# A ring of four activation pairs and gate blocks on ScalarE's queue in the outputs' loop of a hybrid decoder layer

## The chip, the cores and the metric

The kernel runs on one NeuronCore of one Trainium2 chip. The metric is the device time of one execution in microseconds (us); lower is better. The core has TensorE (PE), VectorE (DVE), ScalarE (ACT), GpSimd (POOL) and SyncE (SP), an on-chip memory with 128 partitions, and 16 DMA engines between that memory and the device's main memory.

## What is computed

One layer on 512 tokens of width 1024: a token mixer (gated spatial mixing beside attention), and then PEER, a retrieval of single-neuron experts. The change lies wholly in PEER:

```python
q = (xt @ w_query).reshape(t, PEER_HEADS, 2, D_HALF)
scores = jnp.einsum('thpd,hpnd->thpn', q, sub_keys)
sv, si = lax.top_k(scores, 16)
...                                   # top 16 of the 256 candidates of each of the 8 heads
gate = jax.nn.softmax(top_s, axis=-1)
# a block of 128 tokens, each with 128 chosen experts of 16384
u = jnp.take(expert_u, ii, axis=0)
a = jnp.einsum('ted,td->te', u, xi)
w = gi * jax.nn.gelu(a, approximate=False)
vv = jnp.take(expert_v, ii, axis=0)
out = jnp.einsum('te,ted->td', w, vv)
```

## The kernel before

The 512 tokens are four tiles of 128. One tile (SPARSE, tile 0) is done as the reference says: GpSimd gathers, for each of the 128 selections, one expert row per token (`gather_rows`, 512 KB a gather) into a ring of eight rows; VectorE multiplies and sums the `expert_u` rows with the tokens (`dot`, 128 of them) and later adds the weighted `expert_v` rows into `y` (`add`, 128 of them). A gather starts when the `dot` or `add` of eight rows before has freed its place.

The other three tiles (384 tokens, DTOK) are done densely over all 16384 experts, in 128 products of 128 experts each (m = 0 to 127), BODY = 8 of them a loop body, so 16 bodies (ITERS).

The gates come first: for each token a 128x128 matrix of gates is built by TensorE from one-hot rows (`hot_rows` on VectorE, `gate_rows` and `copy_built` on ScalarE, `build`), 16 tokens a chunk, eight chunks a tile (d = 0, 1, 2), and stored to `gates_dense` in main memory.

The products' loop: SyncE loads 512 KB of `uT` for each product (`load_u`, four ahead). ScalarE rounds it (`u_hi`), VectorE makes the rest (`u_lo`), TensorE makes 24 matmuls, ScalarE's GELU puts the result in `a_out`, and SyncE stores a pair of two products' activations (384 KB) to `gelu_dense` (`store_a`). The first 64 products lie beside the retrieval and the building of the gates; m = 64 to 127 are bodies 8 to 15 of a loop of their own.

The outputs' loop, 128 steps, again eight a body. For step m: `load_v` brings 512 KB of `expert_v` into one of RAW = 4 places; `load_a` brings a pair of activations back (two steps, A_STEPS = 2) into one of two places of `a_block`; `load_g` brings the gates of a whole body (1536 KB, in runs of 512 bytes) into one of two places of `g_block`. VectorE makes `w_raw` = activations x gates (L1580), ScalarE rounds it to `w_hi` (L873) and the expert rows to `v_hi` (L867), VectorE makes `v_lo` (L1583) and `w_lo` (L1587), and TensorE makes 18 matmuls (L1153, L1154, L1157) into six banks that stay open over all 128 steps. After them come the last residual, a norm and the stores of the output.

All orders are written out by hand; each engine waits on semaphores. All of SyncE's loads and stores are issued in one order on its one queue. In `step` on SyncE a body's first act is `load_g` for the next body; then each step issues `load_v` for four steps on, and each odd step `load_a`, which may only fill the place that the step has just freed:

```python
if r == 0 and not first and not last:
    sp.wait_ge(w_made, m)
    load_g(J + 1, 1 - odd)
...
if r % A_STEPS == 1 and not (last and r >= BODY - 3):
    sp.wait_ge(w_made, m + 1)
    load_a(BODY // A_STEPS * J + (r + 3) // A_STEPS, (r + 3) // A_STEPS % 2)
```

The first loads of the outputs' loop are issued in the middle of body 15 of the products' loop. Of the `dot`s, 32 lie beside the chunks of d = 1 and 2 (two a chunk) and 96 in bodies 8 to 13 (two a product). Of the `add`s, 32 lie in bodies 14 and 15 (two a product) and 96 in bodies 0 to 11 of the outputs' loop (one a step).

Of the kernel before, what the change touches and what calls it, by code (L numbers as in the profile page):

```python
# [25 lines left out]
P = 128  # L26
# [113 lines left out]
def program(nc, x, cT, w_ada, b_ada, norm1_g, w_in, b_f, sg_ln_g, sg_ln_b, sg_wT, sg_bT,  # L140
# [5 lines left out]
    with ExitStack() as ctx:  # L146
# [100 lines left out]
        a_block = shared[:, 4 * D:4 * D + 2 * A_STEPS * DTOK].rearrange("p (b i t) -> p b i t", b=2, i=A_STEPS)  # L247
        w_raw = shared[:, 4 * D + 4 * DTOK:4 * D + 6 * DTOK].rearrange("p (b n) -> p b n", b=2)
        w_hi = shared_f32r("w_hi", 4 * D + 6 * DTOK, [P, 2, DTOK])
        w_lo = shared_f32r("w_lo", 4 * D + 8 * DTOK, [P, 2, DTOK])  # L250
# [59 lines left out]
        a_in = [sem(f"a_in{b}") for b in range(2)]  # L310
# [71 lines left out]
        def _(sp):  # L382
# [91 lines left out]
            with sp.Fori(LOOP_AT, ITERS - 1) as I:  # L474
                for r in range(BODY):
                    loop_product(I, r, True)

# [7 lines left out]
            def load_g(q, b):  # L485
                src = g_dram[:, :, bass.ds(q * (G_STEPS * GROUP), G_STEPS * GROUP)]
                sp.dma_start(g_block[:, b].rearrange("p g i t -> p g (i t)"), src.rearrange("g p n -> p g n")).then_inc(g_in[b], 16)
# [34 lines left out]
            for r in range(BODY):  # L522
                step(0, r, 0, True, False)
            with sp.Fori(0, ITERS // 2 - 1) as K:
                for odd in (1, 0):
                    for r in range(BODY):
                        step(2 * K + 2 - odd, r, odd, False, False)
            for r in range(BODY):
                step(ITERS - 1, r, 1, False, True)
# [97 lines left out]
        def _(act):  # L627
# [225 lines left out]

            with act.Fori(LOOP_AT, ADD_AT) as I:
                for r in range(BODY):
                    loop_product(I, r, True)
            act.wait_ge(dot_done, NSEL)
            nc.scalar.activation(act_w[:, :], act_w[:, :], ACT.Gelu).then_inc(gelu_done, 1)
            for I in range(ADD_AT, ITERS):
                for r in range(BODY):  # L860
                    loop_product(I, r, I < ITERS - 1)
# [13 lines left out]
            def step(J, r, first, last):  # L875
# [6 lines left out]
            act.wait_ge(built, DTOK // BATCH)  # L882
# [775 lines left out]
```

## Time and profile before

| | |
|---|---|
| median of 3 runs | 1815.28 us (1812.93 to 1815.53) |
| the profiled execution | 1814.15 us, its span 1812.4 us |
| TensorE busy | 1620.0 us, 89% of the span |
| VectorE, ScalarE, GpSimd busy | 1259.2, 664.0, 390.6 us |
| mean granted TensorE clock | 0.960 of full speed |
| DMA | 426.15 MB, mean 235 GB/s |

The span is the time from the first to the last instruction of the profiled execution; busy times are sums over it. Times of day in the views are microseconds from the start of the span. In it the last products' loop runs from about 902 to 1164, the outputs' loop from 1185.6 to 1794.6.

### The profile page before, as it was taken

What the parts mean: (1) busy time and instruction counts of PE and PEld (TensorE: products, weight loads), DVE (VectorE), ACT (ScalarE), POOL (GpSimd) and SP (SyncE); (2) the same over time, 40 slices, a digit from 0 to 9 for tenths busy, and PEclk for the clock granted to TensorE, in tenths of its full rate; (3) what the DMA queues carried; (4) which work ended last, traced back from release to release, by engine and by line L of the source; (5) the groups of instructions that cost most, each with busy time, mean ns of one, the idle gap of its engine ahead of it and who ended that gap; (6) DMA issues with size and microseconds to landing.
All of it is one profiled execution on the core that took longest, in us unless ns stands there. A gap on an engine that the chain in (4) does not pass through costs nothing.

```text
span 1812.4 us, 23042 instructions
## 1 busy us (share of the span) xinstructions
PE 1620.0 (89%) x7605; PEld 1306.1 (72%) x7605; DVE 1259.2 (69%) x2268; ACT 664.0 (37%) x1227; POOL 390.6 (22%) x326
## 2 busy tenths in 40 slices
PE   1999988999889999999999999688888888989996
PEld 0454565545489889989999999666666676768784
DVE  6457255339977889988888888666666666766556
ACT  2111133212378269438633333132323222323333
POOL 1103200000010003002366666422222222220000
PEclk9889999999989999999999999889999899999998
DMA  9853500000266459647999999988889787887663
GB/s 357 291 187 141 209 1 1 0 0 20 74 204 227 146 178 324 242 150 264 326 412 413 413 413 412 396 281 275 282 294 327 260 268 276 305 281 237 196 213 111
DMA packets 172763, 426.15 MB, mean 235 GB/s; under 512 B 13068, under 2 KB 62220, under 8 KB 169496
## 3 DMA queue, kind: packets, MB, share of 16 engines
q1 hardware_dynamic: 135808, 291.06, 45.3%
q0 software_dynamic: 36864, 134.23, 20.5%
q8 instruction: 35, 0.57, 0.1%
q14 instruction: 32, 0.26, 0.0%
q10 hardware_dynamic: 24, 0.02, 0.0%
HBM read 372.84 MB, written 52.43 MB: 235 GB/s over the span
## 4 chain that ended last, share of the span: by engine, by line
PE 55%; DVE 18%; DMA 13%; SPq 5%; issue 4%; ACT 4%; POOL 1%; DVEq 0%; ACTq 0%; POOLq 0%
PE bank L1153 7%; DMA shared<-gelu_dense 7%; PE bank L1154 7%; PE bank L1157 7%; PE bank L1097 5%; SPq L479 5%; PE bank L1099 5%; PE bank L1098 5%; PE bank L951 5%; PE bank L1026 3%; PE bank L961 3%; PE bank L1112 3%; DMA hT<-in_expert_u,idx_slot 2%; ACT weights L794 2%; DVE u_lo L1486 2%
## 5 line engine op out<-in xcount | busy, mean ns | idle before, releaser
L1153 PE MATMUL bank<-v_hi,w_hi 128*128 128x512 f32 x768 | 310.2, 404 | 81.9 <-DVE w_lo L1587 81.7
L1097 PE MATMUL bank<-h_hi,u_hi 128*128 128x384 f32 x1024 | 348.9, 341 | 23.0 <-DVE u_lo L1486 23.0
L1098 PE MATMUL bank<-h_lo,u_hi 128*128 128x384 f32 x1024 | 345.0, 337 | 0.0
L1099 PE MATMUL bank<-h_hi,u_lo 128*128 128x384 f32 x1024 | 345.0, 337 | 0.0
L1154 PE MATMUL bank<-v_lo,w_hi 128*128 128x512 f32 x768 | 306.6, 399 | 0.0
L867 ACT ACTIVATE v_hi<-weights 128x1024 fp32r<-128x1024 f32 x128 | 135.5, 1059 | 302.7 <-PE bank L1157 249.0
L1157 PE MATMUL bank<-v_hi,w_lo 128*128 128x512 f32 x768 | 242.0, 397 | 0.0
L1153 PEld LDWEIGHTS bank<-v_hi,w_hi 128*128 128x128 f32 x768 | 149.3, 194 | 123.3 <-DVE v_lo L1583 70.0
L1097 PEld LDWEIGHTS bank<-h_hi,u_hi 128*128 128x128 f32 x1024 | 194.4, 190 | 27.3 <-DVE u_lo L1486 16.6
L1583 DVE TENSOR_TENSOR v_lo<-weights,v_hi 128x1024 fp32r<-128x1024 f32 x128 | 156.5, 1222 | 77.3 <-ACT v_hi L867 75.0
L1486 DVE TENSOR_TENSOR u_lo<-weights,u_hi 128x1024 fp32r<-128x1024 f32 x128 | 156.0, 1223 | 66.8 <-PE bank L1099 65.7
L1098 PEld LDWEIGHTS bank<-h_lo,u_hi 128*128 128x128 f32 x1024 | 194.2, 190 | 0.0
L1099 PEld LDWEIGHTS bank<-h_hi,u_lo 128*128 128x128 f32 x1024 | 194.2, 190 | 0.0
L1580 DVE TENSOR_TENSOR shared<-shared,weights 128x384 f32<-128x384 f32 x128 | 71.0, 555 | 156.6 <-DMA shared<-gelu_dense 144.8
L1154 PEld LDWEIGHTS bank<-v_lo,w_hi 128*128 128x128 f32 x768 | 149.4, 195 | 30.8
L1157 PEld LDWEIGHTS bank<-v_hi,w_lo 128*128 128x128 f32 x768 | 148.0, 193 | 31.9
L611 POOL DMA_INDIRECT shared<-in_expert_u,idx_slot x64 | 87.2, 1362 | 314.0 <-DVE shared L1493 290.5
L774 ACT ACTIVATE u_hi<-weights 128x1024 fp32r<-128x1024 f32 x128 | 134.9, 1054 | 0.0
L611 POOL DMA_INDIRECT hT<-in_expert_v,idx_slot x64 | 78.7, 1229 | 207.2 <-DVE y L1499 198.1
L1473 DVE TENSOR_TENSOR weights<-ada 128x1024 f32<-128x1024 f32 x96 | 111.4, 1221 | 16.3 <-ACT ada L824 12.8
L611 POOL DMA_INDIRECT hT<-in_expert_u,idx_slot x64 | 91.4, 1429 | 135.0 <-DVE hT L1493 65.8
L794 ACT ACTIVATE weights<-weights,ada 128x128 f32<-128x128 f32 x384 | 115.2, 389 | 14.2 <-DVE weights L1473 14.2
(233 smaller groups left out, 2195.9 us busy)
## 6 DMA issues: line engine op xcount, KB each, us to landing
weights<-in_uT SPq DMA_DIRECT2D x128, 512.0 KB
weights<-in_expert_v SPq DMA_DIRECT2D x128, 512.0 KB, 4.8
weights<-in_w_ada SPq DMA_DIRECT2D x12, 2048.0 KB, 9.6
gates_dense<-weights SPq DMA_DIRECT2D x24, 1024.0 KB, 6.4
shared<-gelu_dense SPq DMA_DIRECT2D x64, 384.0 KB
weights<-gates_dense SPq DMA_DIRECT2D x16, 1536.0 KB, 13.4
gelu_dense<-weights SPq DMA_DIRECT2D x32, 384.0 KB
gelu_dense<-final_row SPq DMA_DIRECT2D x32, 384.0 KB
```

The costliest lines, as they stand in the source:

```text
L611: nc.gpsimd.indirect_dma_start(ring(r % ROWS), None, table, bass.IndirectOffsetOnAxis(idx_slot[:, half, r:r + 1], 0))\
L774: nc.scalar.activation(u_hi[:, r % RAW, :], u_raw[:, r % RAW, :], ACT.Copy).then_inc(u_hi_made, 1)
L794: ins = nc.scalar.activation(rows, rows, ACT.Copy, scale=turned[:, half * HTOK // P % 2, 2, token:token + 1])
L867: nc.scalar.activation(v_hi[:, r % 2, :], v_raw[:, r % RAW, :], ACT.Copy).then_inc(v_hi_made, 1)
L1097: nc.tensor.matmul(a, uh[:, k, :], h2_hi[:, :, k, :], start=(k == 0), stop=False)
L1098: nc.tensor.matmul(a, uh[:, k, :], h2_lo[:, :, k, :], start=False, stop=False)
L1099: ins = nc.tensor.matmul(a, ul[:, k, :], h2_hi[:, :, k, :], start=False, stop=(k == KC - 1))
L1153: nc.tensor.matmul(acc, wh, v_hi[:, r % 2, cols], start=begin, stop=False)
L1154: nc.tensor.matmul(acc, wh, v_lo[:, r % RAW, cols], start=False, stop=False)
L1157: ins = nc.tensor.matmul(acc, wl, v_hi[:, r % 2, cols], start=False, stop=end)
L1486: tt(u_lo[:, r % LOW, :], u_raw[:, r % RAW, :], u_hi[:, r % RAW, :].bitcast(F32), ALU.subtract).then_inc(u_lo_made, 1)
L1583: tt(v_lo[:, r % RAW, :], v_raw[:, r % RAW, :], v_hi[:, r % 2, :].bitcast(F32), ALU.subtract).then_inc(v_lo_made, 1)
```

## The change

It has four parts. (1) `a_block` becomes a ring of four pairs (A_RING = 4), so a pair is loaded four pairs (a whole body) ahead of its use; `w_raw`, `w_hi` and `w_lo` move to other addresses to make room. (2) `load_g` moves from SyncE's queue to ScalarE's: in the outputs' loop ScalarE issues it at the start of a body, ahead of its rounding of `w`. (3) The first loads (four of `expert_v`, four pairs, two gate blocks) are issued in body 14, two bodies ahead of the outputs' loop. (4) The work for the sparse tile is spread anew: 48 `dot`s beside all three tiles' chunks, 64 in bodies 8 to 11 (two a product), 16 in bodies 12 and 13 (one a product), none in body 14; eight `add`s in body 15 (one a product) and 120 in bodies 0 to 14 of the outputs' loop (one a step), where `add` now stands between `w_raw` and `v_lo`.

```diff
-DOTS_AT = {1: 0, 2: 2 * CHUNKS}
-DOTS_IN_CHUNKS = 4 * CHUNKS
-ADD_AT = 14
-ADDS_IN_LOOP = 2 * BODY * (ITERS - ADD_AT)
+DOTS_IN_CHUNKS = 6 * CHUNKS
+FEW_DOTS_AT, DOTS_END, ADD_AT = 12, 14, 15
+ADDS_IN_LOOP = BODY * (ITERS - ADD_AT)
+A_RING = 4
...
-        a_block = shared[:, 4 * D:4 * D + 2 * A_STEPS * DTOK].rearrange("p (b i t) -> p b i t", b=2, i=A_STEPS)
-        w_raw = shared[:, 4 * D + 4 * DTOK:4 * D + 6 * DTOK].rearrange("p (b n) -> p b n", b=2)
+        a_block = shared[:, 4 * D:4 * D + A_RING * A_STEPS * DTOK].rearrange("p (b i t) -> p b i t", b=A_RING, i=A_STEPS)
+        w_raw = ada[:, 2 * D:2 * D + 2 * DTOK].rearrange("p (b n) -> p b n", b=2)
...
 SyncE
-            for r in range(RAW):
-                loop_product(ITERS - 1, r, True)
+            with sp.Fori(LOOP_AT, DOTS_END) as I:
+                for r in range(BODY):
+                    loop_product(I, r, True)
             wait_full(sp, "turn", DENSE - 1)
             for b in range(2):
-                sp.wait_ge(g_stored[b], 16 * GROUPS // 2)
-                sp.wait_ge(a_stored[b], 16)
-            load_v(0, 0)
-            load_a(0, 0)
-            load_g(0, 0)
-            for n in range(1, RAW):
-                load_v(n, n)
-            load_a(1, 1)
-            for r in range(RAW, BODY):
-                loop_product(ITERS - 1, r, False)
-            load_g(1, 1)
+                sp.wait_ge(a_stored[b], 16 * A_RING // 2)
+            for r in range(BODY):
+                loop_product(DOTS_END, r, True)
+                if r < RAW:
+                    load_v(r, r)
+                else:
+                    load_a(r - RAW, r - RAW)
+            for r in range(BODY):
+                loop_product(ITERS - 1, r, r < RAW)
...
-            def step(J, r, odd, first, last):
+            def step(J, r, last):
                 m = BODY * J + r
-                if r == 0 and not first and not last:
-                    sp.wait_ge(w_made, m)
-                    load_g(J + 1, 1 - odd)
+                if r % A_STEPS == 1 and not last:
+                    sp.wait_ge(w_made, m + 1)
+                    load_a(BODY // A_STEPS * (J + 1) + r // A_STEPS, r // A_STEPS)
                 if not (last and r >= RAW):
                     sp.wait_ge(v_used, m + 1)
                     load_v(m + RAW, r)
-                if r % A_STEPS == 1 and not (last and r >= BODY - 3):
-                    sp.wait_ge(w_made, m + 1)
-                    load_a(BODY // A_STEPS * J + (r + 3) // A_STEPS, (r + 3) // A_STEPS % 2)
...
 ScalarE
+            for b in range(2):
+                act.wait_ge(g_stored[b], 16 * GROUPS // 2)
+            act.wait_ge(built, DTOK // BATCH)
+            for r in range(BODY):
+                if r % RAW == 0:
+                    load_g(r // RAW, r // RAW)
+                loop_product(DOTS_END, r, True)
+                if r == 0:
+                    act.wait_ge(dot_done, NSEL)
+                    nc.scalar.activation(act_w[:, :], act_w[:, :], ACT.Gelu).then_inc(gelu_done, 1)
+            for r in range(BODY):
+                loop_product(ITERS - 1, r, False)
...
-            def step(J, r, first, last):
+            def step(J, r, odd, first, last):
+                if r == 0 and not first and not last:
+                    load_g(J + 1, 1 - odd)
                 round_w(J, r, first and r < 2)
...
 VectorE, beside the chunks
-                    if d in DOTS_AT:
-                        for q in range(2):
-                            at = DOTS_AT[d] + 2 * c + q
-                            dve.wait_ge(gathered[at % ROWS], 16 * (at // ROWS + 1))
-                            dot(at, at)
+                    for q in range(2):
+                        at = 2 * (d * CHUNKS + c) + q
+                        dve.wait_ge(gathered[at % ROWS], 16 * (at // ROWS + 1))
+                        dot(at, at)
...
 VectorE, step of the outputs' loop
                 if r % A_STEPS == 0:
-                    dve.wait_ge(a_in[r // A_STEPS % 2], 16 * (BODY // A_STEPS // 2 * J + r // A_STEPS // 2 + 1))
+                    dve.wait_ge(a_in[r // A_STEPS], 16 * (J + 1))
...
                    g_block[:, odd, :, r, :], ALU.mult).then_inc(w_made, 1)
+                if adding:
+                    loop_add(J, r)
...
-                if adding:
-                    n = BODY * J + ADDS_IN_LOOP + r
-                    dve.wait_ge(gathered[r % ROWS], 16 * ((NSEL + ADDS_IN_LOOP) // ROWS + 1 + BODY // ROWS * J))
-                    add(n, r)
```

## Rows read from the trace of the kernel before

**Rows 1.** Busy time of each engine in stretches, with clock and DMA

```profile
core 0: us, PE busy (x) PEld busy (x) DVE busy (x) ACT busy (x) POOL busy (x), PEclk, DMA share, GB/s
1185.60:1794.60 609.00, 548.34 (x2304) 444.19 (x2304) 390.63 (x479) 195.25 (x256) 115.08 (x98) 0.95 0.77 261
902.00:1164.40 262.40, 259.91 (x1493) 258.30 (x1492) 221.00 (x281) 87.10 (x122) 172.84 (x139) 1.00 1.03 409
1164.40:1185.60 21.20, 0.00 (x0) 0.00 (x0) 2.76 (x5) 3.17 (x5) 2.23 (x3) 0.58 1.07 367
1143.00:1173.00 30.00, 20.74 (x117) 19.71 (x115) 18.52 (x15) 4.16 (x6) 14.04 (x14) 0.91 1.04 393
1226.40:1589.42 363.02, 313.27 (x1298) 252.69 (x1297) 240.56 (x288) 109.97 (x145) 94.70 (x81) 0.93 0.84 286
1349.50:1386.97 37.47, 34.98 (x146) 27.91 (x145) 26.70 (x32) 12.36 (x17) 10.70 (x9) 0.95 0.92 310
1670.24:1704.17 33.93, 32.55 (x144) 26.67 (x143) 17.39 (x24) 11.78 (x17) 0.00 (x0) 1.00 0.66 214
1704.17:1737.23 33.06, 32.91 (x145) 26.95 (x144) 17.46 (x24) 12.13 (x17) 0.00 (x0) 1.00 0.68 222
```

**Rows 2.** Chain of waits, the last 12 steps of the outputs' loop

```profile
1745.39 0.47 PE bank L1153
...
1794.15 0.47 PE bank L1157 x2
```

**Rows 3.** Waits from 1185.6 to 1794.6: total us, times, longest

```profile
DVE shared L1580 <- DMA shared<-gelu_dense: 144.8, 52, 8.6
...
PE bank L1153 <- DVE w_lo L1587: 81.7, 24, 21.3
...
ACT v_hi L867 <- DMA weights<-in_expert_v: 53.5, 11, 6.6
```

**Rows 4.** Timeline of SyncE's queue, 1223 to 1236: start, us, what

```profile
1223.39 0.40 SPq L487 DMA_DIRECT2D weights<-gates_dense  x1
...
1232.87 0.38 SPq L482 DMA_DIRECT2D shared<-gelu_dense  x1
```

**Rows 5.** The first load issued behind a gate block (L479), at two places

```profile
L479 SPq DMA_DIRECT2D weights<-in_expert_v x1: 5662/5662/5662, 1226.4 to 1226.4; - x1
...
L479 SPq DMA_DIRECT2D weights<-in_expert_v x1: 27654/27654/27654, 1143.6 to 1143.6; - x1
```

**Rows 6.** ScalarE's timeline between the loops

```profile
1182.34 0.49 ACT L782 ACTIVATE final_row<-bank 128x384 f32<-128x384 f32 x1 [26.44 <-DMA gelu_dense<-final_row]
```

**Rows 7.** Issue to landing: gate blocks 1220 to 1640, then v loads 1300 to 1640

```profile
DMA to landing us min/median/max: 10.5/13.5/14.1
...
DMA to landing us min/median/max: 3.4/5.4/9.6
```

**Rows 8.** DMA queues, 1143 to 1173: packets, MB, share of the engines' time

```profile
q0 software_dynamic: 2396, 8.69, 73.9%
q1 hardware_dynamic: 3055, 3.11, 30.0%
```

**Rows 9.** Groups of instructions in the outputs' loop

```profile
L1583 DVE TENSOR_TENSOR v_lo<-weights,v_hi 128x1024 fp32r<-128x1024 f32 x127 | 155.2, 1222 | 70.6 <-ACT v_hi L867 68.3 <-issue 2.2
...
L867 ACT ACTIVATE v_hi<-weights 128x1024 fp32r<-128x1024 f32 x126 | 133.4, 1059 | 302.7 <-PE bank L1157 249.0 <-DMA weights<-in_expert_v 53.5
...
L1587 DVE TENSOR_TENSOR w_lo<-shared,w_hi 128x384 fp32r<-128x384 f32 x127 | 70.0, 551 | 0.0
```

**Rows 10.** VectorE's timeline, the first and last product beside chunks, d = 0 and 1

```profile
519.65 1.23 DVE L1486 TENSOR_TENSOR u_lo<-weights,u_hi 128x1024 fp32r<-128x1024 f32 x1 [1.21 <-PE bank L1099]
...
575.30 1.23 DVE L1486 TENSOR_TENSOR u_lo<-weights,u_hi 128x1024 fp32r<-128x1024 f32 x1 [1.61 <-PE bank L1099]
...
667.92 1.23 DVE L1486 TENSOR_TENSOR u_lo<-weights,u_hi 128x1024 fp32r<-128x1024 f32 x1 [1.21 <-PE bank L1099]
...
728.58 1.23 DVE L1486 TENSOR_TENSOR u_lo<-weights,u_hi 128x1024 fp32r<-128x1024 f32 x1
```

More of the change, by code:

```diff
@@ L309, in program @@
         a_stored = [sem(f"a_stored{b}") for b in range(2)]
[L310 removed]
+        a_in = [sem(f"a_in{b}") for b in range(A_RING)]
         x_in, c_in, small_in, norm1_in = sem("x_in"), sem("c_in"), sem("small_in"), sem("norm1_in")
@@ L517, in step @@
                     load_v(m + RAW, r)
-                if r % A_STEPS == 1 and not (last and r >= BODY - 3):
-                    sp.wait_ge(w_made, m + 1)
-                    load_a(BODY // A_STEPS * J + (r + 3) // A_STEPS, (r + 3) // A_STEPS % 2)
+            with sp.Fori(0, ITERS - 1) as J:
+                for r in range(BODY):
+                    step(J, r, False)
             for r in range(BODY):
[L523 to L529, printed above, removed]
+                step(ITERS - 1, r, True)
             for t in range(NT):
@@ L1542, in _, with loop_product @@
                             hot_rows(HALVES * (d * CHUNKS + c + 1) + h)
-            def loop_product(I, r, more, adding):
+            def loop_product(I, r):
                 if r + 1 < BODY:
                     rest_of_u(I, r + 1)
-                elif more:
+                elif not (isinstance(I, int) and I == ITERS - 1):
                     rest_of_u(I + 1, 0)
-                for q in range(2):
-                    at = 2 * r + q
-                    if adding:
-                        n = 2 * BODY * (I - ADD_AT) + at
-                        dve.wait_ge(gathered[at % ROWS], 16 * (NSEL // ROWS + 2 * BODY // ROWS * (I - ADD_AT) + at // ROWS + 1))
-                        add(n, at)
-                    else:
-                        n = 2 * BODY * (I - LOOP_AT) + DOTS_IN_CHUNKS + at
-                        dve.wait_ge(gathered[at % ROWS], 16 * (2 * BODY // ROWS * (I - LOOP_AT) + DOTS_IN_CHUNKS // ROWS + at // ROWS + 1))
-                        dot(n, at)
@@ L1560, in _, with loop_dot @@
[L1560 to L1570 removed]
+            def loop_dot(before, I, at):
+                dve.wait_ge(gathered[at % ROWS], 16 * (before // ROWS + I + at // ROWS + 1))
+                dot(BODY * I + before + at, at)
@@ new lines, in loop_add @@
+            def loop_add(J, r):
+                dve.wait_ge(gathered[r % ROWS], 16 * ((NSEL + ADDS_IN_LOOP) // ROWS + 1 + J))
+                add(BODY * J + ADDS_IN_LOOP + r, r)
+            with dve.Fori(LOOP_AT, FEW_DOTS_AT) as I:
+                for r in range(BODY):
+                    loop_product(I, r)
+                    for q in range(2):
+                        loop_dot(DOTS_IN_CHUNKS - 2 * BODY * LOOP_AT, 2 * I, 2 * r + q)
+            before = DOTS_IN_CHUNKS + 2 * BODY * (FEW_DOTS_AT - LOOP_AT)
@@ new lines, in _ @@
+            for I in range(FEW_DOTS_AT, DOTS_END):
+                for r in range(BODY):
+                    loop_product(I, r)
+                    loop_dot(before, I - FEW_DOTS_AT, r)
+            for r in range(BODY):
+                loop_product(DOTS_END, r)
+                if r == 2:
+                    dve.wait_ge(gelu_done, 1)
+                    tt(act_w[:, :], act_w[:, :], gate_sparse[:, :], ALU.mult).then_inc(w_ready, 1)
+                    dve.wait_ge(dot_done, NSEL)
+                    dve.wait_ge(w_ready, 1)
+                    nc.vector.memset(y[:, SPARSE, :], 0.0).then_inc(v_added, 1)
@@ L1572, in step @@
+            for r in range(BODY):
+                loop_product(ITERS - 1, r)
+                loop_add(-1, r)
             def step(K, odd, r, first, adding):
@@ L1600, in _ @@
                         step(K, odd, r, False, True)
-            with dve.Fori(adding_bodies // 2, ITERS // 2) as K:
-                for odd in range(2):
-                    for r in range(BODY):
-                        step(K, odd, r, False, False)
+            for odd in range(2):
+                for r in range(BODY):
+                    step(ITERS // 2 - 1, odd, r, False, odd == 0)
             def finish(t):
```

47 lines of the change are left out of this document (15 added, 32 removed).

## Prediction

> **What bounds the kernel now.** I read the busy times by stretch first, because the share of TensorE over the whole span (89%) hides where it idles. In the outputs' loop TensorE is busy 548.3 of 609.0 us, at a mean granted clock of 0.95; in bodies 8 to 15 of the products' loop 259.9 of 262.4; between the two loops it does nothing for 21.2 us [rows 1]. So there are three places, and the outputs' loop is the large one.
>
> What would the loop take with nothing in the way? Its last 12 steps follow on one another: 1745.39 to 1794.15 + 0.47 is 49.2 us, or 4.10 us a step [rows 2]. 128 steps are 525 us, a body of eight 32.8. The loop takes 84 us more: 61 of idle TensorE, and 23 because matmuls behind a stall run at the lower clock. Nine bodies in a row, all with additions and a gate block each, take 363.0 us, 40.3 each; two late bodies without additions take 33.9 and 33.1 [rows 1].
>
> The waits tell what comes last. VectorE waits 144.8 us for `shared<-gelu_dense`, a pair of activations; behind that TensorE waits for `w_lo` (81.7 us, of which 21.3 are the gap between the loops). A second wait runs beside it: ScalarE waits 53.5 us for rows of `expert_v`, 11 times, up to 6.6 us [rows 3].
>
> Why is the pair late? SyncE's queue shows it. The gate block is issued at 1223.39 in 0.40 us. The next load, of `expert_v`, comes 3.0 us later at 1226.40 and its issue takes 5.66 us; only at 1232.87, behind one more, goes the pair out [rows 4, 5]. The block takes 13.5 us to land [rows 7], and the pair is behind it. With two places, no pair can be issued earlier. At the turn of the loops the same thing is larger: with gathers two a product the load behind the first block stands for 27.65 us [rows 5], all of SyncE's stores stand behind it, and ScalarE waits 26.4 us until `gelu_dense<-final_row` has landed and `final_row` may be written again [rows 6].
>
> **The change, part by part.**
>
> *Ring of four pairs.* A pair is issued as soon as its place is free, eight steps (32.8 us) ahead. Even the late pairs of before would have landed 20 us early. That takes away the wait for `gelu_dense`. What is late next is the load of `expert_v`, issued only when its place is free: the place of step m is freed at the end of m, and ScalarE wants the new rows at the end of step m + 2, two steps or 8.2 us later. They land in 5.4 us at the median, 9.6 at most [rows 7].
>
> *Gate block on ScalarE's queue.* On ScalarE the issue costs some 0.40 us, once a body, ahead of `w_hi`. `v_lo` (1.22 us) is being made meanwhile, longer than the 0.40 us, so I cost it at nothing; without that cover it is 14 x 0.4 = 6 us. Behind it on ScalarE stand `w_hi` and the next `v_hi`, and TensorE waits for both. What the block does to SyncE's loads is the open price. If the load behind it was held by its own queue alone, that cost goes to zero. If what holds it is shared by both queues, the load of `expert_v` is still held. No row of before shows a block on another queue. Bounds: a body of 32.8 us from below; from above one with a late load, worked out under the rivals. I take 33.9 us, the slower of the two late bodies [rows 1]. Independently, the engines' DMA share gives the same: 0.84 x 363.0 / 9 = 33.9 us of DMA time a body with additions [rows 1]. The bytes alone would allow less: eight rows' loads and eight gathers of 0.524 MB, four pairs of 0.393 and a block of 1.57 are 11.5 MB, at the 393 GB/s of the stretch 1143 to 1173 29.3 us [rows 1].
>
> The loop then: blocks are fetched in bodies 1 to 14, 14 x 33.9 + 2 x 32.8 = 540.2 us, against 609.0: **-68.8**. The additions are still one a step and VectorE has room for them: 26.8 us of 32.8 at the rate of the nine bodies (240.6 / 9 [rows 1]). That 24 more of them lie here costs only through the DMA time, which the 33.9 holds for all bodies. In the new place `add` comes before `v_lo`: it fills the time in which ScalarE makes `v_hi`, and costs something only where its gather is late.
>
> *First loads two bodies ahead.* Loads for steps 0 to 3 and both blocks have 33 us and more. The last product takes 4.1 us; meanwhile ScalarE's last but one GELU (0.49), `v_hi` (1.06), `v_lo` (1.22) and `w_lo` (0.55) [rows 6, 9] come to 3.3 us, so TensorE goes on nearly without a gap. I leave 1 us of 21.2: **-20.2**. The price is body 14. It moves eight `uT` rows, four of `expert_v`, four pairs out and four in, and two blocks: 12 x 0.524 + 8 x 0.393 + 2 x 1.57 = 12.6 MB in 33 us, 381 GB/s, when 409 is what the loop moved [rows 1]. ScalarE issues the second block 16 us behind the first; if the first is not far enough, ScalarE stands, and with it GELU and `u_hi`, of which some 6 us are hidden by products made ahead. SyncE's `uT` loads are four products ahead. **+2**, bounds 0 and 12.
>
> *Fewer gathers late in the products' loop.* Eight fewer `dot`s or `add`s a body from body 12 on. The loop idles 2.5 us now [rows 1], part of it at the turn from `dot` to `add`, which stays. **-1.2**, bounds 0 and -2.5.
>
> *Sixteen `dot`s beside the chunks of d = 0.* This part costs. A chunk without `dot`s takes (575.30 - 519.65) / 7 = 7.95 us, with two (728.58 - 667.92) / 7 = 8.67 [rows 10]. Eight chunks: 8 x 0.72 = **+5.8**. Bounds 0 (if the one-hot building on ScalarE is the pace) and 16 x 1.22 = 19.5.
>
> Sum: -68.8 - 20.2 + 2 - 1.2 + 5.8 = -82.4, so a span of 1812.4 - 82.4 = 1730.0. This execution took 1.75 us outside its span, 1731.8; the median of the runs is 1.1 above it: **1733 us**, 4.5% less.
>
> **A rule weighed against the rows.** Where two queues have work, the rows 1143 to 1173 show how they share: gathers in 2396 packets and the rest, mostly pieces of the block, in 3055, while the megabytes are 8.69 to 3.11 [rows 8]; so it is by packet, not by byte. The Trainium skill (DMA: Bandwidth & Descriptors, Queues, rings and completion order) says that a DMA engine takes turns between queues a packet at a time; by this rule, the trace agrees, the block on a third queue gets small turns and lands later than 13.5 us, but it delays each packet of the others only by one short one. With 33 us to land, the sum stays.
>
> **Rivals.**
>
> *A. Both queues share what makes the issues wait.* The block is issued on ScalarE about 1.2 us into a step (behind `v_hi`), the path stays taken until 8.7 us after the issue (0.40, 3.0 and 5.66 us make 1223.39 to 1232.06 [rows 4, 5]), that is 9.9 us into it. The load of `expert_v` due at 4.2 goes out then, lands 5.4 later at 15.3, and `v_hi`, `v_lo`, `w_lo` end at 18.2 with the hand-overs, when TensorE wants it at 16.4: 1.9 us late. With a landing of 9.6 it is 6.1. For: the second wait [rows 3] shows such loads late even now. Against: in those cases they also stood behind the block's bytes in one queue. With 1.9 to 6.1 and the low clock behind it, say 3.6 a body, the loop is 525 + 50 = 575, and body 14 some 6 instead of 2: 1812.4 - 34 - 20.2 - 1.2 + 5.8 + 6 + 2.9 = **1772 us**. 
>
> *B. The DMA engines are the bound.* The highest share that a body with additions reached is 0.92 (1349.5 to 1387.0 [rows 1]), so 33.9 / 0.92 = 36.8 us: 15 x 36.8 + 32.8 = 585, hence -24: 1812.4 - 24 - 20.2 - 1.2 + 5.8 + 2 + 2.9 = **1778 us**. For: 0.84 busy at a 40.3 us body. Against: 409 GB/s at a share of 1.03 in the products' loop.
>
> *C. Nothing left in the way.* Bodies of 33.0: 528, body 14 free: **1718 us**.
>
> *D. Slower than before.* ScalarE itself stands at each block until the first two thirds are out, as SyncE's next issue does (8.7 us). `w_hi` then comes at 9.9 us, `w_lo` at 11.2, and TensorE stands 7 us a body and loses 2 more at the low clock: 525 + 14 x 9.4 = 657, and body 14 with two such waits +20: 1812.4 + 48 - 20.2 - 1.2 + 5.8 + 20 + 2.9 = **1868 us**. It decides from about 7 us lost a body. Against: issuing the block took 0.40 us, it was the next one that stood.
>
> **How the numbers follow.** Chances: the forecast (bodies about 33.9, 1724 to 1748) 0.42, A 0.24, B 0.08, C (below 1724) 0.18, D 0.04; 0.04 for something not seen. The forecast's own range is 1724 to 1748. The range over the cases is 1708 to 1772: the low end is C with no cost of body 14 and chunks that hide half of the `dot`s, the high end is the middle of A. A measurement here can tell 0.2% (3.6 us) from no change. All but D and a little of the rest are faster: faster 0.94, same 0.02, slower 0.04.
>
> **What the profile after would show.** Waits for `shared<-gelu_dense` on VectorE gone; between the loops no gap above 2 us; bodies of the outputs' loop 33 to 35 us at a DMA share near 1; nothing on SyncE held 5 us. If A is right, each body has one issue of `expert_v` of 5 us or more just behind ScalarE's block, and ScalarE waits for `weights<-in_expert_v`. If B is right, the block's landing nears 33 us and VectorE waits for `weights<-gates_dense`. If D is right, the issue on ScalarE's queue is long. Chunks of d = 0 should stand 8.7 us apart. The prediction is wrong if the loop's body stays above 37 us or ScalarE loses its lead in body 14.

## The result, and the profile after

The changed kernel takes **1709.07 us** (median of 4, 1705.92 to 1710.63) against 1815.4 before in the same comparison: ratio 0.941, 95% interval 0.9385 to 0.9433, 5.9% faster. The prediction was 1733 with a range of 1708 to 1772. The direction and the mechanism held; the gain is 24 us larger than forecast, and the time lies only 1 us above the low end of the range.

The spans are 1812.4 and 1705.9 us, 106.5 apart. The windows of the changed kernel show where they went (columns as in [rows 1]):

```profile
core 0: us, PE busy (x) PEld busy (x) DVE busy (x) ACT busy (x) POOL busy (x), PEclk, DMA share, GB/s
1163.80:1688.00 524.20, 522.92 (x2306) 432.26 (x2304) 418.87 (x501) 189.63 (x257) 188.40 (x125) 1.00 0.92 326
902.00:1163.80 261.80, 261.80 (x1512) 261.80 (x1511) 180.48 (x234) 91.47 (x128) 113.42 (x100) 1.00 0.97 366
1200.00:1600.00 400.00, 398.91 (x1761) 330.13 (x1760) 327.52 (x390) 144.37 (x195) 165.27 (x110) 1.00 0.99 353
```

The outputs' loop takes 524.2 us where it took 609.0 [rows 1], with TensorE busy in 522.9 of them and the clock at full speed. That is 32.8 us a body, the floor that the prediction read from [rows 2]. It begins at 1163.8, in the same microsecond in which the products' loop ends; the 21.2 us between the loops are gone. The products' loop itself has no idle microsecond left.

The waits from 1170 to 1680 hold no line for `gelu_dense` any more. The wait for rows of `expert_v` is left, smaller than the 53.5 us of [rows 3] and spread over more times. The two lines beneath it are what TensorE waited for in the whole loop, the first before a load of weights, the second before a matmul:

```profile
ACT v_hi L866 <- DMA weights<-in_expert_v: 44.7, 15, 4.7
```

```profile
  DVE v_lo L1595: 2.1, 2
  DVE w_lo L1599: 1.3, 2
```

Of ScalarE's 44.7 us almost nothing reaches TensorE, which is idle for 1.3 of the loop's 524.2 us: rows that come while ScalarE and VectorE still have time in a step cost nothing.

The loads in the loop, landing in us, answer to [rows 7]: first the gate blocks on ScalarE's queue with their issues, then the rows of `expert_v` with theirs from 1200 to 1680.

```profile
L843 ACTq DMA_DIRECT2D weights<-gates_dense x16: 379/401/441, 1093.6 to 1618.9; - x16
...
DMA to landing us min/median/max: 15.6/27.0/28.8
...
L475 SPq DMA_DIRECT2D weights<-in_expert_v x116: 327/333/339, 1200.9 to 1671.8; - x116
...
DMA to landing us min/median/max: 3.1/6.2/10.2
```

A block now lands in 27.0 us instead of 13.5 and has 33. No issue of `expert_v` takes over 0.339 us, where the one behind a block took 5.7 [rows 5]. The queues from 1200 to 1600 (packets, MB, share):

```profile
q1 hardware_dynamic: 21101, 70.50, 47.0%
q0 software_dynamic: 14098, 51.33, 34.6%
q10 hardware_dynamic: 37774, 19.24, 16.9%
```

q10 is ScalarE's queue. It has half of the packets and a seventh of the bytes.

The remaining part of the difference lies before the loop. TensorE's turns of the gates (the last of three transposes, one a tile d) are good marks. Before, then after:

```profile
510.70 0.27 PE L921 MATMUL bank<-ident,gate 128*128 128x128 f32 x1
658.97 0.27 PE L921 MATMUL bank<-ident,gate 128*128 128x128 f32 x1
815.47 0.27 PE L921 MATMUL bank<-ident,gate 128*128 128x128 f32 x1
```

```profile
507.51 0.27 PE L922 MATMUL bank<-ident,gate 128*128 128x128 f32 x1
662.15 0.27 PE L922 MATMUL bank<-ident,gate 128*128 128x128 f32 x1
818.69 0.27 PE L922 MATMUL bank<-ident,gate 128*128 128x128 f32 x1
```

The first mark is 3.2 us earlier though nothing ahead of it changed; over all runs of this study it lies between 506.5 (e2) and 511.8 (e1), so this is scatter. From the first to the second, where the 16 `dot`s were added, it takes 154.6 instead of 148.3 us: +6.4. From the second to the third 156.5 both times. From there to the end of the products' loop (1164.4, then 1163.8) 345.1 instead of 348.9: -3.8. In sum -3.2 + 6.4 - 3.8 - 21.2 - 84.8 = -106.6, which is the 106.5 of the spans within rounding.

### The profile page after: what moved, and what is told of

It reads as the page before. It is cut to its first block, busy times and chain, and to the rows that moved or that the text cites. A ratio compares the mean times of both kernels' runs of the same rounds, so it can differ in the third digit from the quotient of the medians.

```text
span 1705.9 us, 22939 instructions
## 1 busy us (share of the span) xinstructions
PE 1591.9 (93%) x7605; PEld 1291.6 (76%) x7605; DVE 1258.1 (74%) x2268; ACT 658.8 (39%) x1227; POOL 424.5 (25%) x326
## 4 chain that ended last, share of the span: by engine, by line
PE 72%; DVE 18%; ACT 5%; DMA 3%; issue 2%; ACTq 0%; DVEq 0%; SPq 0%
PE bank L1154 10%; PE bank L1158 10%; PE bank L1155 10%; PE bank L1098 8%; PE bank L1100 8%; PE bank L1099 8%; PE bank L952 5%; PE bank L1027 3%; PE bank L962 3%; ACT weights L781 3%; DVE u_lo L1487 2%; PE bank L1044 2%; DVE weights L1474 2%; DVE ada L1403 1%; PE bank L1113 1%
## 5 line engine op out<-in xcount | busy, mean ns | idle before, releaser
L1154 PE MATMUL bank<-v_hi,w_hi 128*128 128x512 f32 x768 | 298.9, 389 | 1.3 <-DVE w_lo L1599 1.3
L1155 PE MATMUL bank<-v_lo,w_hi 128*128 128x512 f32 x768 | 298.8, 389 | 0.0
L1158 PE MATMUL bank<-v_hi,w_lo 128*128 128x512 f32 x768 | 236.6, 389 | 0.0
L1154 PEld LDWEIGHTS bank<-v_hi,w_hi 128*128 128x128 f32 x768 | 144.2, 188 | 31.7 <-DVE v_lo L1595 2.1
L1155 PEld LDWEIGHTS bank<-v_lo,w_hi 128*128 128x128 f32 x768 | 144.2, 188 | 29.9
L1158 PEld LDWEIGHTS bank<-v_hi,w_lo 128*128 128x128 f32 x768 | 144.2, 188 | 29.9
L598 POOL DMA_INDIRECT hT<-in_expert_v,idx_slot x64 | 107.3, 1677 | 159.1 <-DVE y L1500 143.2
L598 POOL DMA_INDIRECT shared<-in_expert_v,idx_slot x64 | 94.9, 1483 | 188.7 <-DVE y L1500 170.2
```

Of the source, the lines that this page charges most:

```text
L598: nc.gpsimd.indirect_dma_start(ring(r % ROWS), None, table, bass.IndirectOffsetOnAxis(idx_slot[:, half, r:r + 1], 0))\
L1154: nc.tensor.matmul(acc, wh, v_hi[:, r % 2, cols], start=begin, stop=False)
L1155: nc.tensor.matmul(acc, wh, v_lo[:, r % RAW, cols], start=False, stop=False)
L1158: ins = nc.tensor.matmul(acc, wl, v_hi[:, r % 2, cols], start=False, stop=end)
```

## The experiments

Ratios are to the kernel before, run on the same chip in the same job. The loop is the outputs' loop, from the start of its first to the end of its last matmul; the gap is TensorE's idle time ahead of it. Both come from one profiled execution of each run, while the median is over four to six.

| run | median us (range) | ratio, 95% | loop us | gap us |
|---|---|---|---|---|
| before | 1815.4 | | 609.0 | 21.3 |
| after | 1709.07 (1705.92 to 1710.63) | 0.941 (0.9385 to 0.9433) | 524.2 | 0 |
| e1, blocks on SyncE | 1744.37 (1740.51 to 1752.68) | 0.959 (0.9564 to 0.9624) | 564.8 | 0 |
| e2, blocks on ScalarE alone | 1785.33 (1782.65 to 1794.69) | 0.984 (0.9799 to 0.9874) | 586.4 | 21.3 |
| e3, no first dots | 1711.01 (1709.27 to 1712.83) | 0.942 (0.9398 to 0.9442) | 523.9 | 0 |
| e4, first loads later | 1710.44 (1708.29 to 1712.77) | 0.942 (0.9393 to 0.9438) | 524.8 | 0 |
| e5, two blocks at once | 1708.49 (1707.88 to 1709.92) | 0.943 (0.9397 to 0.946) | 523.8 | 0 |
| e6, no first dots, late GELU | 1711.37 (1708.96 to 1712.49) | 0.944 (0.9416 to 0.9465) | 523.0 | 0 |
| e7, old spread | 1727.10 (1724.98 to 1730.08) | 0.953 (0.9505 to 0.9556) | 525.8 | 3.8 |
| e8, two more loads | 1743.75 (1739.50 to 1746.21) | 0.961 (0.958 to 0.9648) | 558.5 | 0 |
| e9, second block later | 1704.36 (1700.36 to 1705.92) | 0.940 (0.9384 to 0.9424) | 523.7 | 0 |
| e10, one dot a chunk | 1700.43 (1699.74 to 1704.22) | 0.938 (0.936 to 0.9402) | 524.7 | 0 |
| e11, add behind w_lo | 1707.82 (1706.21 to 1711.79) | 0.943 (0.9404 to 0.9449) | 524.6 | 0 |
| e12, first loads as before | 1723.13 (1722.88 to 1724.34) | 0.949 (0.9471 to 0.951) | 526.9 | 10.5 |

**Queue or ring: e1 and e2.** The first takes the changed kernel and puts the loop's gate blocks back on SyncE; the second takes the kernel before and only moves them to ScalarE.

```diff
 e1, on the changed kernel, SyncE's step
+                if r == 0 and not first and not last:
+                    sp.wait_ge(w_made, m)
+                    load_g(J + 1, 1 - odd)
 and ScalarE's step
-                if r == 0 and not first and not last:
-                    load_g(J + 1, 1 - odd)
...
```

> The changed kernel with one part undone: inside the outputs' loop the gate blocks are issued on SyncE's queue again, as before; the ring of four pairs, the early first loads (their two blocks still on ScalarE's queue) and the new spread stay. Theory Q (the queue is what counts): the load of expert_v due behind a block is held some 5.7 us and then lies behind the block's bytes, so it lands some 5 us late in each of 14 bodies, with the low clock behind it: 1709 + 14 x 3 to 14 x 5, 1750 to 1780 us, ScalarE waiting for weights<-in_expert_v more than 80 us, no wait for gelu_dense. Theory R (the ring is what counts, the only thing late was the pair): 1709 to 1718 us.

e1 measured 1744.37 us, 35 more than the changed kernel. Theory R falls: with pairs in hand eight steps ahead there is still a loss. Theory Q named the right load and too large a size: its range began at 1750. The timeline of SyncE's queue shows the same hold as before, 3.38 us at this place and up to 5.8 in the loop, the waits name who pays, and no wait for `gelu_dense` is left:

```profile
1202.24 0.40 SPq L503 DMA_DIRECT2D weights<-gates_dense  x1
1205.78 3.38 SPq L475 DMA_DIRECT2D weights<-in_expert_v  x1
```

```profile
ACT v_hi L874 <- DMA weights<-in_expert_v: 114.7, 28, 7.0
```

```diff
 e2, on the kernel before, SyncE's step
-                if r == 0 and not first and not last:
-                    sp.wait_ge(w_made, m)
-                    load_g(J + 1, 1 - odd)
 and ScalarE's step
+                if r == 0 and not first and not last:
+                    load_g(J + 1, 1 - odd)
                 round_w(J, r, first and r < 2)
...
```

> The kernel before with one part of the change alone: inside the outputs' loop the gate blocks are issued on ScalarE's queue; two places for pairs, first loads and spread as before. A pair is then issued some 10 us before its use and should land in 7.4 us. Theory Q: the loop comes down by 60 to 75 us, to 1740 to 1755 us, body 33 to 35 us, the gap of 21 us between the loops stays. Theory R: pairs stay late because two places are too few, 1790 to 1815 us.

e2 measured 1785.33, just below theory R's range, and the loop came down by 22.6 us only. No issue of `expert_v` is held any more (0.347 us at most) and ScalarE's wait for these rows is gone, but VectorE's wait for pairs stays:

```profile
DVE shared L1584 <- DMA shared<-gelu_dense: 129.3, 55, 6.7
```

and a pair lands in 6.3 us at the median:

```profile
shared<-gelu_dense SPq DMA_DIRECT2D x39, 384.0 KB, 6.3
```

I had counted 10 us from issue to use. Count it again: the pair goes out behind the row of `expert_v` at the end of an odd step; two more steps follow, 8.2 us, and the step after them uses it. Its `w_raw` (0.55), then `v_lo` (1.22, with `w_hi` beside it) and `w_lo` (0.55) must be over when that step begins. Of 8.2 us some 5.5 are left, with the issues taken off, and 6.3 is more. So with two places the pair is late even when nothing is held.

Each part takes away its own wait. The queue alone gives 22.6 us of the loop's 84.8. The rest of the change without it (e1 against before) gives 44.1, and that is the ring: e7 and e12 below undo the new spread and the early first loads, and the loop stays at 526 to 527 us. The last 18 would come of both together, but they rest on single executions, and that of e1 is the slowest of its four, 8.3 us above the median. The blocks' queue is worth 23 us on the kernel before and 41 on the changed one by these loops, but 30 and 34 us, each to about 7, by the ratios of the times. So the times show no gain that needs both parts; whether there is one stays open. No run has the ring alone on the kernel before.

**The turn of the loops: e4, e12, e7, e5.**

```diff
 e4: the first loads in body 15
             for r in range(BODY):
-                loop_product(DOTS_END, r, True)
+                loop_product(ITERS - 1, r, r < RAW)
                 if r < RAW:
                     load_v(r, r)
                 else:
                     load_a(r - RAW, r - RAW)
... the SyncE loop ahead of it runs one body more, and ScalarE issues its two blocks in body 15
```

> The changed kernel with the first loads (four of expert_v, four pairs, two blocks) issued in body 15 instead of 14, one body ahead. If what closed the gap is that nothing is held behind the first block in SyncE's queue and that the gathers are fewer, one body ahead is enough: the first block lands in 25 us and the gap stays under 2 us: 1707 to 1711 us. Rival: the distance closed it; then TensorE stands some 5 to 15 us between the loops: 1714 to 1725 us.

1710.44 us, no gap, and TensorE is idle for 1.5 us in the whole loop. One body ahead is enough.

```diff
 e12: the first loads as before, on SyncE's queue
+            for r in range(RAW):
+                loop_product(ITERS - 1, r, True)
...
+            load_v(0, 0)
+            load_a(0, 0)
+            load_g(0, 0)
+            for n in range(1, RAW):
+                load_v(n, n)
+            for n in range(1, A_RING):
+                load_a(n, n)
+            for r in range(RAW, BODY):
+                loop_product(ITERS - 1, r, False)
+            load_g(1, 1)
...
```

> The changed kernel with only the first loads as before: in the middle of body 15, all on SyncE's queue, the first block behind the first rows and the first pair, the other loads and the stores behind the block; inside the outputs' loop the blocks stay on ScalarE's queue, ring and spread stay. Theory (the gap of 21 us came of the block standing ahead of the last stores in SyncE's queue): ScalarE again waits for gelu_dense<-final_row, TensorE stands 8 to 20 us between the loops, less than before since there are half as many gathers beside the block: 1716 to 1730 us. Rival (with fewer gathers the block is out in time and distance and queue do not matter): 1707 to 1712 us.

1723.13 us, 14 more. The timelines of SyncE's queue, ScalarE and TensorE at the turn:

```profile
1145.40 0.71 SPq L483 DMA_DIRECT2D weights<-gates_dense  x1
1146.16 11.55 SPq L475 DMA_DIRECT2D weights<-in_expert_v  x3
...
1159.17 0.43 SPq L442 DMA_DIRECT2D gelu_dense<-final_row  x1
...
1160.12 0.43 SPq L483 DMA_DIRECT2D weights<-gates_dense  x1
```

```profile
1174.56 0.49 ACT L778 ACTIVATE final_row<-bank 128x384 f32<-128x384 f32 x1 [15.01 <-DMA gelu_dense<-final_row]
```

```profile
1177.87 0.77 PE L1161 MATMUL bank<-v_hi,w_hi 128*128 128x512 f32 x1 [10.52 <-DVE w_lo L1606]
```

It is the picture of [rows 5, 6] at about half size: of the three rows behind the block the first is held for 10.6 us, where it was 27.65; the stores stand behind them, and ScalarE waits 15.0 us for `final_row`. The block itself lands in 16.4 us instead of 33.4. That this is so because half as many gathers run beside it is argued, not tested. The second body is not needed (e4). e4 and e12 differ in the queue of the blocks and in the half body by which the loads come earlier, and no run takes these two apart.

```diff
 e7: the old spread of dots and adds
-DOTS_IN_CHUNKS = 6 * CHUNKS
-FEW_DOTS_AT, DOTS_END, ADD_AT = 12, 14, 15
-ADDS_IN_LOOP = BODY * (ITERS - ADD_AT)
+DOTS_IN_CHUNKS = 4 * CHUNKS
+FEW_DOTS_AT, DOTS_END, ADD_AT = 14, 14, 14
+ADDS_IN_LOOP = 2 * BODY * (ITERS - ADD_AT)
...
```

> The changed kernel with the old spread of the sparse tile's work: 32 dots beside chunks, two dots a product in bodies 8 to 13, two adds a product in bodies 14 and 15, one a step in bodies 0 to 11 of the outputs' loop. Body 14 then wants 12.6 MB and 16 gathers of 0.524 MB, 21 MB in 33 us, where 413 GB/s give 13.6. Theory (the spread is needed so that the first loads find room): loads of uT and gathers late, TensorE stands 15 to 25 us in bodies 14 and 15: 1718 to 1735 us. Rival (the bodies of the outputs' loop gain from four gather-free bodies and the chunks' 6 us come back): 1703 to 1712 us.

1727.10 us, inside the theory's range. Body 14 is full, but much of the loss came by a way that I had not named in this place. ScalarE's timeline with its queue:

```profile
1109.51 16.71 ACTq L843 DMA_DIRECT2D weights<-gates_dense  x1
1126.27 0.49 ACT L769 ACTIVATE final_row<-bank 128x384 f32<-128x384 f32 x1 [15.40 <-issue]
```

The second block's issue stands 16.7 us, ScalarE with it, and TensorE waits 9.2 us for that GELU. Late rows of `uT` (16.9 us of ScalarE's waits) come on top. The run also puts the GELU of `act_w` ahead of the first product of body 14, where ScalarE waits 6.2 us for the last `dot`s and TensorE 2.3 behind it; so it is not the spread alone.

```diff
 e5: both first blocks one behind the other
-                if r % RAW == 0:
-                    load_g(r // RAW, r // RAW)
+                if r == 0:
+                    load_g(0, 0)
+                    load_g(1, 1)
```

> The changed kernel, but in body 14 ScalarE issues the second gate block directly behind the first instead of four products later. Theory (what stands is the next issue on the same queue, until about two thirds of the block before it are out): the second issue takes some 15 us, ScalarE has about 6 us to spare, TensorE stands about 10 us in body 14: 1715 to 1725 us, and SyncE's issues beside it stay at 0.3 to 0.5 us. Rival (a queue takes two blocks, and what stood behind the block was particular to SyncE): the second issue takes 0.4 us and the time stays at 1706 to 1712 us.

1708.49 us: no cost that the times show. The mechanism is there and its size was misjudged. ScalarE's queue, and SyncE's at the same time:

```profile
1092.89 0.41 ACTq L843 DMA_DIRECT2D weights<-gates_dense  x1
1093.34 8.28 ACTq L843 DMA_DIRECT2D weights<-gates_dense  x1
```

```profile
1093.98 0.34 SPq L439 DMA_DIRECT2D weights<-in_uT  x1
```

The second issue stands 8.3 us, not 15. The first block lands in 14.0 us here, with less beside it: from 1093 to 1102 the gathers move 0.91 MB and SyncE's queue 0.90, and the block 1.14. In e6, below, they move 1.91 and 1.50 in the same stretch, and the block gets 0.22. ScalarE's lead hides all but 1.4 us, which TensorE waits. The last line is the one that answers rival A: while ScalarE stands at its issue, SyncE issues a load in 0.34 us. In e3 and e7 it does so too, in 0.33 us. ScalarE's hold is its own queue's and does not reach SyncE's.

**The sparse tile's work: e3, e6, e9, e10, e11.**

```diff
 e3: no dots beside the chunks of d = 0
-FEW_DOTS_AT, DOTS_END, ADD_AT = 12, 14, 15
+FEW_DOTS_AT, DOTS_END, ADD_AT = 14, 14, 15
...
-                    for q in range(2):
-                        at = 2 * (d * CHUNKS + c) + q
+                    for q in range(2 if d else 0):
+                        at = 2 * ((d - 1) * CHUNKS + c) + q
```

> The changed kernel with the 16 dots beside the chunks of d = 0 moved: none there, and bodies 12 and 13 of the products' loop take two a product instead of one. Chunks of d = 0 then stand 7.95 us apart instead of 8.67, which gives 5.8 us; if the two added saturated bodies cost nothing: 1703 us. Rival: the gathers fall behind at 413 GB/s, the last dot is late, and GELU of act_w holds ScalarE and with it the products: 1709 us or more.

1711.01 us. The chunks do give 7 us (the third mark lies at 811.7 instead of 818.7), and the stretch from there to the outputs' loop takes 354.1 instead of 345.1, which loses them again.

```diff
 e6: e3, and GELU of act_w three products later
-                if r == 0:
+                if r == 3:
                     act.wait_ge(dot_done, NSEL)
...
```

> The kernel without dots beside the chunks of d = 0 (two a product up to body 13 instead), and ScalarE's GELU of act_w three products later in body 14 (behind product 3), VectorE's use of it behind product 5. Without this delay the 7 us won in the chunks were lost again around the turn of bodies 13 and 14, where ScalarE waited 8 us for the last dots. Theory (ScalarE's wait is what lost them): 1703 to 1706 us. Rival (the gathers themselves are late, VectorE stands at the last dots and makes u_lo late): 1708 to 1712 us.

1711.37 us: the theory was wrong. The time is the rival's, but its mechanism is not: VectorE waits 1.3 us at most for a gather in body 14. The theory rested on a wait misread: in e3 ScalarE waits 2.1 us for the last `dot`s, not 8, and the wait of 8.7 is VectorE's for `u_hi`. ScalarE's timeline of e6 has the cause, which e3 shows too (11.43 us):

```profile
1109.14 10.96 ACTq L843 DMA_DIRECT2D weights<-gates_dense  x1
...
1120.15 0.49 ACT L769 ACTIVATE final_row<-bank 128x384 f32<-128x384 f32 x1 [9.76 <-issue]
```

In the changed kernel the same issue at 1110.03 takes 0.39 us. With gathers at two a product up to body 13 the first block lands in 35.1 us instead of 27.3; it is not out far enough when the second is issued 18.7 us later, and ScalarE stands there. e9 moves that one issue.

```diff
 e9: e3, and the second block in body 15
-                if r % RAW == 0:
-                    load_g(r // RAW, r // RAW)
+                if r == 0:
+                    load_g(0, 0)
                 loop_product(DOTS_END, r, True)
...
             for r in range(BODY):
+                if r == 4:
+                    load_g(1, 1)
                 loop_product(ITERS - 1, r, False)
```

> No dots beside the chunks of d = 0 (two a product up to body 13 instead), and the second gate block issued in the middle of body 15 instead of body 14. In the two kernels without those dots ScalarE stood some 11 us at the issue of the second block, because the first had not gone out far enough between the late gathers, and TensorE stood behind it. Theory (that issue lost the 7 us of the chunks): the issue takes 0.4 us, the products' loop ends near 1156, 1700 to 1704 us. Rival (something else of the saturated bodies, late u loads or gathers, costs the same): 1708 to 1712 us.

```profile
1086.27 0.41 ACTq L843 DMA_DIRECT2D weights<-gates_dense  x1
1136.59 0.39 ACTq L843 DMA_DIRECT2D weights<-gates_dense  x1
```

Both issues (ScalarE's queue) take 0.4 us, the outputs' loop begins at 1157.1 instead of 1163.8, and the median is 1704.36 us, at the upper edge of the theory's range. From the first mark to the end of the span e9 takes 1698.6 - 507.1 = 1191.5 us, the changed kernel 1705.9 - 507.5 = 1198.4: the chunks' 7 us are there.

```diff
 e10: e9, with dots of the chunks one a chunk for d = 0 and 1
-                    for q in range(2 if d else 0):
-                        at = 2 * ((d - 1) * CHUNKS + c) + q
+                    for q in range((1, 1, 2)[d]):
+                        at = (c, CHUNKS + c, 2 * CHUNKS + 2 * c + q)[d]
```

> The kernel with the second block later, and the 32 dots beside the chunks placed one a chunk for d = 0 and 1 and two a chunk for d = 2. Two dots a chunk cost 0.72 us a chunk. Theory (the chunk is near VectorE's limit only with two; one is hidden behind ScalarE's gate rows): eight chunks give 5 to 6 us more, 1695 to 1699 us. Rival (each dot costs the same 0.4 us): no difference from the kernel with two for d = 1 and 2, 1700 to 1704 us.

```profile
511.63 0.27 PE L924 MATMUL bank<-ident,gate 128*128 128x128 f32 x1
662.43 0.27 PE L924 MATMUL bank<-ident,gate 128*128 128x128 f32 x1
814.23 0.27 PE L924 MATMUL bank<-ident,gate 128*128 128x128 f32 x1
```

Marks of e10. With no (e9), one and two (the changed kernel) `dot`s a chunk the stretch of d = 0 takes 147.6, 150.8 and 154.6 us, so the first eight `dot`s cost 3.2 and the second eight 3.8: nearly linear, the rival's side. From the first mark to the end it is 1190.9 us against e9's 1191.5. The median of 1700.43 is 3.9 below e9's, but the two ranges overlap, and the marks say that the code gained less than 1. Both are faster than the changed kernel by a little, judged by e11, which times like it and ran in the same job: e11's fastest execution (1706.21) lies above the slowest of e9 (1705.92) and of e10. By the intervals of the ratios only e10 stands clear, by a hair (it ends at 0.9402, e11 begins at 0.9404); those of e9 and e11 overlap.

```diff
 e11: add behind w_lo
-                if adding:
-                    loop_add(J, r)
                 dve.wait_ge(v_hi_made, m + 1)
...
+                if adding:
+                    loop_add(J, r)
```

> The changed kernel with add at its old place, behind w_lo, in a step of the outputs' loop. Theory (VectorE has 6 of 32.8 us a body to spare and the order does not matter): 1707 to 1712 us, no more waits of TensorE. Rival (add before w_raw of the next step makes w_hi late by its 1.28 us whenever the pace is full): 1715 to 1740 us.

1707.82 us, no difference that the times show. Where `add` stands in the step does not matter at this pace.

**How near to the bound: e8.**

```diff
 e8: two more loads of 512 KB a body
+                if not last and r % RAW == 2:
+                    b = r // RAW
+                    sp.wait_ge(idle_in[b], 16 * (J + 1))
+                    sp.dma_start(slot(1)[:, b * D:(b + 1) * D], expert_v[bass.ds(m * P, P), :]).then_inc(idle_in[b], 16)
...
```

> The changed kernel with work added: two more loads of 512 KB a body of the outputs' loop on SyncE's queue, into a place that nobody reads. A body then moves 12.6 MB instead of 11.5. Theory (the engines' share of 0.99 means that they are full): the body grows by 9%, 2.9 us, 15 bodies: 1745 to 1755 us. Rival (what limits is bytes, 413 GB/s, and 12.6 MB in 32.8 us are 384): 1709 to 1718 us, gate blocks landing later than 27 us but within 33.

1743.75 us, just below the theory's range; the rival falls. The loop grows by 34 us, 6.5%, for 9% more bytes. The window from 1200 to 1600, and the waits for loads in the loop:

```profile
1200.00:1600.00 400.00, 381.20 (x1648) 311.21 (x1647) 306.89 (x366) 135.42 (x182) 144.61 (x104) 0.99 0.99 357
```

```profile
ACT v_hi L874 <- DMA weights<-in_expert_v: 65.5, 20, 6.3
...
DVE ada L1598 <- DMA weights<-gates_dense: 15.0, 5, 5.0
```

The engines' share is 0.99 as without the added loads, and the bytes rise from 353 to 357 GB/s only. So in this loop, with a seventh of the bytes in 512-byte pieces, no run moves more than 357 GB/s, though the products' loop, which has no such pieces, moves 409 [rows 1]. That the pieces are what makes the difference is likely, and no run varies them alone. Part of the added time may be order in SyncE's queue, where the added loads stand among the rows of `expert_v`; that was not taken apart.

## Why the prediction was right, and what it had wrong

**What bounds the kernel, and the floor.** Right. The 84 us of the loop and the 21 between the loops were there to be had, and the floor of 32.8 us a body was reached.

**Ring of four pairs.** Right as a mechanism: the wait for `gelu_dense` is gone, and the load of `expert_v` is what comes late next, by e1 and by the 44.7 us of ScalarE's waits. The prediction gave the two parts one sum, and so did not say that the ring is the larger: 44 of the loop's 85 us come without the blocks' new queue (e1), 23 with the queue alone (e2).

**Gate block on ScalarE's queue.** Here lies the miss. "I take 33.9 us" for bodies 1 to 14 was 1.1 too much; the body takes 32.8, and the loop gave 84.8 instead of 68.8. Both supports of 33.9 were weak. The late bodies of [rows 1] still had two places for pairs (VectorE waits 17.9 us for `gelu_dense` between 1670 and 1737), so their loss was one that the change takes away. And the DMA time of 0.84 x 40.3 = 33.9 us did not stay: at the pace after, the same bytes take 0.99 x 32.8 = 32.5 us. It was only 4% too large, but that is the whole distance between a body that the DMA sets and one that TensorE sets; why it shrank no run shows. The bound from the bytes at 393 GB/s was too low on the other side: at the 357 GB/s of e8 the 11.5 MB take 32.3 us. The case that came is rival C, to which the prediction gave 0.18: 1718 us, still 9 more than measured.

**First loads two bodies ahead.** -20.2 forecast, -21.2 measured. The price in body 14, +2, was not there: no issue stood and TensorE idled nowhere. e3, e5, e6 and e7 show how near it was: ScalarE's hold is 8 to 17 us when the first block is not out far enough.

**Fewer gathers late.** -1.2 forecast, -3.8 measured from the third mark to the end of the products' loop; the idle 2.5 us went, and about 1 us is within what marks scatter.

**Dots beside the chunks.** +5.8 forecast, +6.4 measured.

In sum: 16.0 (loop) + 1.0 (gap) + 2 (body 14) + 2.6 (late gathers) + 3.2 (scatter ahead of the first mark) - 0.6 (chunks) = 24.2, which is the miss within rounding.

**The range.** That 1709 lies in it is partly luck. The low end, 1708, is called C with a free body 14 and half of the `dot`s hidden, but C's sum has body 14 free already, and 1718.7 - 2.9 is 1716. The result lies below that, because the loop, the gap and the late gathers all came out at or below their floors and 3.2 us are scatter ahead of the first mark. The main range, 1724 to 1748, missed.

**Rivals.** A is refuted by e5 (SyncE issues in 0.34 us while ScalarE stands) and by the changed kernel itself, in which no issue of `expert_v` is held. D's mechanism is real, but only where the second block comes early: 0.4 us behind the first in e5, or 19 to 21 us behind it beside many gathers in e3, e6 and e7. In the loop they are 33 us apart, and a block lands in 27.

**The rule weighed.** Turns by packet (the Trainium skill, DMA: Bandwidth & Descriptors, Queues, rings and completion order): the trace after agrees as far as it goes. The block, now alone in a queue of many small packets, takes twice as long, 27.0 us, and the rows of `expert_v` only 6.2 instead of 5.4. The pace of the loop changed too, so this is no test by itself. A plainer one is e6 from 1102 to 1110, where all three queues have work; the gathers, SyncE's queue and ScalarE's block move (packets, MB, share)

```profile
q0 software_dynamic: 416, 1.52, 47.0%
q1 hardware_dynamic: 419, 1.49, 47.0%
q10 hardware_dynamic: 419, 0.21, 9.5%
```

The same number of packets each, and for the block a seventh of the bytes of either other. e7 shows the same from 1110 to 1126 (841, 840 and 840 packets). This fits the block's slow landing beside gathers.

## What to carry to other kernels

A large load of small pieces (here 1536 KB in 512-byte runs; its size and its pieces were not varied apart) delays everything behind it on its queue twice, by its bytes and by holding the next issue. Give it a queue of its own, and leave it time there before the next large load, since the engine that issues it stands otherwise: here an issue 16.4 us behind a block that lands in 27.3 went through, and one 18.7 us behind a block that lands in 35.1 stood for 11 us. Count the slack of a prefetch from its issue to the moment at which its last consumer must be done, not to its first use: the 10 us that I gave the two-place ring were some 5.5. When a change has two parts, undo each on the new kernel and try each alone on the old. Compare the two prices over several executions before you say that the parts need each other: the queue came to 30 and 34 us by the times, and to 23 and 41 by the loops of single profiled executions.

## What the runs showed of the hardware

An issue on a queue is held while a large earlier transfer of the same queue is under way: 5.7 us for the load behind a block of 3072 pieces in the loop before, 27.7 us beside dense gathers, 8.3 to 16.7 us on ScalarE's queue. It goes on when most of the time that the block takes to land has passed (8.7 of 14.0 us in e5, 29.6 of 35.1 in e6). While ScalarE's queue was held, SyncE's was not (0.33 to 0.34 us in e3, e5 and e7). With work on three queues each moved as many packets (416, 419 and 419 in 8 us of e6, 841, 840 and 840 in 16 us of e7), whatever their size, so the queue with 512-byte pieces got a seventh of the bytes of either other. With a seventh of its bytes in 512-byte pieces the DMA reached 357 GB/s at a busy share of 0.99, against 409 in the products' loop, which has none. The DMA time that a body of the outputs' loop needs, share times length, came down from 33.9 to 32.5 us for the same bytes when the stalls went.
